# A hybrid decoder block on one core: the gate columns of the input projection as seven token-major half products, handed on through DRAM

## The reference

```python
h = rmsnorm(x, mix_pre_g)
proj = h @ w_in                       # 2048 -> 1024 + 1024 | 1024 | 4096
a_in, b_in, gates = split(proj)       # GLU input | pooling input | gates of both branches
a = a_val * sigmoid(a_gate)           # then causal depthwise conv, 31 taps
a = silu(layernorm(conv(a)))
y_a = a @ w_a_out                     # 1024 -> 2048
mixed = per-group linear map of (trailing mean - token) of b_in
y_b = (mixed * pool_scale) @ w_b_out  # 1024 -> 2048
merged = sigmoid(gates_a) * y_a + sigmoid(gates_b) * y_b
x = x + rmsnorm(merged @ w_o, mix_post_g)
...
```

## Time and profile before

| | us |
|---|---|
| runs | 2543.63, 2544.37, 2546.49 |
| median | 2544.37 |
| profiled execution, its span | 2544.4 |
| TensorE busy in it | 2498.3 (98%) |
| VectorE, ScalarE, GpSimd busy | 1922.4, 1053.4, 193.7 |

### The profile page before, as it was taken

How to read it: one execution, slowest core, us unless ns; L and a number is a source line. 1 busy time by engine, 2 the same in 40 slices (tenths; PEclk the granted TensorE clock), 3 DMA queues, 4 the chain that set the end, 5 groups by cost and what they waited for, 6 DMA issues and landing times. The chain is left out here.

```text
span 2544.4 us, 35985 instructions
## 1 busy us (share of the span) xinstructions
PE 2498.3 (98%) x14180; PEld 2193.4 (86%) x14180; DVE 1922.4 (76%) x2289; ACT 1053.4 (41%) x1224; POOL 193.7 (8%) x273
## 2 busy tenths in 40 slices
PE   9999999999999999999999999999999999999998
PEld 7788888888888787899999999999987878877886
DVE  7888766653335788889989998899988787788434
ACT  5222322252224445444444444444454453455323
POOL 0000000000000000011111111011111111200000
PEclk9999999999999999999999999999999999999999
DMA  4322333234334564467777776777787777976221
GB/s 170 106 101 91 100 99 99 91 123 134 99 99 148 166 216 181 152 196 207 211 187 213 215 218 204 195 207 210 222 269 238 262 237 192 278 228 226 89 99 67
DMA packets 155602, 435.48 MB, mean 171 GB/s; under 512 B 13504, under 2 KB 49344, under 8 KB 154432
## 3 DMA queue, kind: packets, MB, share of 16 engines
q1 hardware_dynamic: 120400, 304.12, 34.4%
q0 software_dynamic: 32656, 124.80, 20.3%
q10 hardware_dynamic: 2400, 4.53, 0.5%
HBM read 396.44 MB, written 36.96 MB: 170 GB/s over the span
## 5 line engine op out<-in xcount | busy, mean ns | idle before, releaser
L1259 ACT ACTIVATE w_hi<-ring_raw 128x1024 fp32r<-128x1024 f32 x426 | 450.6, 1060 | 606.6 <-PE ps L1144 388.0
L1762 DVE TENSOR_TENSOR ring_lo<-ring_raw,w_hi 128x1024 fp32r<-128x1024 f32 x426 | 518.6, 1222 | 190.5 <-ACT w_hi L1259 188.5
L873 PE MATMUL ps<-xg_hi,w_hi 128*128 128x512 f32 x1024 | 401.3, 392 | 7.7 <-DVE w_lo L1721 4.1
L1721 DVE TENSOR_TENSOR w_lo<-w_raw,w_hi 128x1024 fp32r<-128x1024 f32 x160 | 195.1, 1223 | 282.5 <-ACT w_hi L1239 282.3
L874 PE MATMUL ps<-xg_lo,w_hi 128*128 128x512 f32 x1024 | 399.6, 390 | 0.0
L875 PE MATMUL ps<-xg_hi,w_lo 128*128 128x512 f32 x1024 | 399.6, 390 | 0.0
L1142 PE MATMUL ps<-s_hi,w_hi 128*128 128x256 f32 x1280 | 362.3, 283 | 2.4 <-issue 2.4
L1144 PE MATMUL ps<-s_hi,ring_lo 128*128 128x256 f32 x1280 | 362.5, 283 | 0.0
L1143 PE MATMUL ps<-s_lo,w_hi 128*128 128x256 f32 x1280 | 362.1, 283 | 0.0
L1239 ACT ACTIVATE w_hi<-w_raw 128x1024 fp32r<-128x1024 f32 x160 | 168.8, 1058 | 390.3 <-PE ps L875 353.9
L1142 PE MATMUL ps<-xg_hi,w_hi 128*128 128x256 f32 x960 | 271.2, 282 | 0.6 <-DVE ring_lo L1762 0.6
(11 more groups left out here) (284 smaller groups left out, 4360.8 us busy)
## 6 DMA issues: line engine op xcount, KB each, us to landing
ring_raw<-in_w_up SPq DMA_DIRECT2D x200, 512.0 KB, 4.7
ring_raw<-in_w_down SPq DMA_DIRECT2D x114, 512.0 KB, 4.5
w_raw<-in_w_in SPq DMA_DIRECT2D x110, 512.0 KB, 3.2
ring_raw<-in_w_up POOLq DMA_DIRECT2D x80, 512.0 KB, 5.9
out_raw<-in_w_o SPq DMA_DIRECT2D x48, 512.0 KB, 4.2
ring_raw<-in_w_ple_gate SPq DMA_DIRECT2D x32, 512.0 KB, 3.5
xd_raw<-gx_dram POOLq DMA_DIRECT2D x14, 1024.0 KB, 10.6
gx_dram<-g_sums POOLq DMA_DIRECT2D x44, 256.0 KB, 7.9
```

The lines of the kernel that those rows point to most:

```text
L873: pe.matmul(o, w_hi[:, s, cols], hi, start=start, stop=False)
L1259: f(w_hi[:, (U_S + n) % SLOTS], raw_of(n), ACT.Copy).then_inc(hi_ready, 1)
L1721: dve.tensor_tensor(w_lo[:, s], w_raw[:, u.slot(RAW)], as_f32(w_hi[:, s]), ALU.subtract).then_inc(lo_ready, 1)
L1762: dve.tensor_tensor(low_of_unit(n), raw_of(n), as_f32(w_hi[:, (U_S + n) % SLOTS]), ALU.subtract).then_inc(lo_ready, 1)
```

## The change

The 4096 gate columns are taken out of `w_in` as `w_gates`, laid out like `w_o`. They are computed in four groups (`GATE_GROUPS`) of two column blocks of 512 with the seven products over halves of the contraction, of the columns and of the tokens: per group 28 units (7 products by 4 units of K), each of 12 token-major matmuls. The two units of the pooled map stand after the first four. The operand sums of x (`x_sum`) are made in place in `xt_raw`, scaled by ScalarE in stage B (`scale_x`) and split into `xs_hi`, `xs_lo`. The weight sums T1, T2, T3 are made by GpSimd with `tensor_tensor` over 128x1024 (for the first group T1 by a DMA that adds), T4 by VectorE. VectorE puts the products together in `gate_parts` (six operations per group), ScalarE takes sigmoids with the row factor `rstd_x` as scale and stores 512 KB pieces in `gates_dram` through its own DMA queue; the result of the pooled map goes through `mixed_dram`. Then come the two branch products, token-major: side 0 (B) and side 1 (A), each four column blocks of four units of 24 matmuls. VectorE multiplies each block by gates read back by GpSimd's queue (1 MB each) into `mtok`, and TensorE transposes `mtok` back (64 transposes of 128x128), which ScalarE copies to `merged`. Nothing changes from the out stage on except where in the list of the first 14 units VectorE's and ScalarE's sums stand, and which semaphores are used.

```diff
-U_B = U_A + 4 * HC
-U_M1 = U_B + 2 * HC + 2
...
+def gate_units(h):
+
+    if h == 0:
+        units = [(GATE, h, W11, q) for q in range(4)] + [(POOLED, n) for n in range(2)]
+        units += [(GATE, h, W21, q) for q in range(4)] + [(GATE, h, mat, q) for q in range(4) for mat in (T1, T2, T4)]
+    else:
+        units = [(GATE, h, mat, q) for q in range(4) for mat in ((W11, T1, T2, T4) if q < 3 else (W11, T2, T1, T4))]
+        units += [(GATE, h, W21, q) for q in range(4)]
+    return units + [(GATE, h, mat, q) for q in range(4) for mat in (T3, W22)]
...
+MIX_HOME = [j % GATE_RING if j < N_GATES else (j - N_GATES) % BRANCH_RING for j in range(N_MIX)]
...
 @block.sync
+            def mix_free(j):
+
+                home, before = MIX_HOME[j], MIX_BEFORE[j]
+                if before is not None:
+                    sp.wait_ge(units_done, U_M + before + 1)
...
 @block.gpsimd
+            def gate_sums(h, q):
+
+                first = gate_landed(h, T1, q)
+                if h == 0:
+                    pool.wait_ge(first_gate_added[q], 16)
+                else:
+                    pool.tensor_tensor(first, first, gate_landed(h, W11, q), ALU.add).then_inc(gate_sum, 1)
+                    pool.wait_ge(gate_sum, gate_summed(h, T1, q))
+                second = gate_landed(h, T2, q)
+                pool.tensor_tensor(second, second, first, ALU.add).then_inc(gate_sum, 1)
...
+            for k in range(4):
+                pool.wait_ge(gate_out[k], 16 * (GATE_GROUPS if k < 2 else 2))
+            gates_back(0, 0)
+            gates_back(0, 1)
...
 @block.tensor
+                for kk in range(2):
+                    k, cols = 2 * q + kk, slice(kk * W, (kk + 1) * W)
+                    for b in range(2):
+                        hi, lo = gate_x(mat, k, slice(b * P, (b + 1) * P))
+                        o = ps[:, bank + b]
+                        pe.matmul(o, hi, w_hi[:, s, cols], start=k == 0 and not onto, stop=False, skip_group_check=onto)
+                        pe.matmul(o, lo, w_hi[:, s, cols], start=False, stop=False, skip_group_check=onto)
+                        mm = pe.matmul(o, hi, w_low[:, cols], start=False, stop=k == HC - 1, skip_group_check=onto)
...
+            def turn_branch(n):
+
+                pe.wait_ge(mtok_ready, BLK * (n + 1))
+                for q in range(4):
+                    for b in range(BLK):
+                        mm = pe.transpose(ps[:, 4 * (n % 2) + q, b * P:(b + 1) * P], mtok[:, n, b, q * P:(q + 1) * P], ident[:])
...
 @block.scalar
+            def x_sum_high(k):
+
+                half, tok = ((upper, far), (lower, near), (lower, far), (upper, near))[k]
+                if half == lower:
+                    for n in range(2):
+                        act.wait_ge(mixed_out[n], 16)
...
 @block.vector
+                if c >= 4:
+                    x_sum(c - 4)
...
+                if j >= N_GATES - 4:
+                    mixed_low(j - N_GATES + 4)
+                elif j >= end_of_map + 4 and tap < 3 * CONV_W:
+                    conv_taps(HC // 2 + 1 + tap // CONV_W, tap % CONV_W, tap % CONV_W + 1)
+                    tap += 1
...
-            out_sum_2()
-            step(At(U_O - 1))
-            out_sum_1()
             for j in range(O_UNITS - 2):
...
-                if j == 1:
+                if j == 2:
+                    out_sum_2()
+                if j == 3:
+                    out_sum_1()
+                if j == 4:
                     late_low(near, 1)
```

More of the change, by code:

```diff
@@ L444, in build @@
         ple_taken, y_ready = sem("ple_taken"), sem("y_ready")
-        x_back, x2_out = [sem(f"x_back{k}") for k in range(2)], sem("x2_out")
+        x2_out = sem("x2_out")
         x2_in = [sem(f"x2_in{n}") for n in range(NG)]
@@ L1021, in _, with gate_x @@
-            with pe.Fori(1, 3) as i:
-                for j in range(4):
-                    branch(At(U_M1 + 3 * j, i, 12), At(T_M1 + 2 * j, i, 8), mixed_hi, mixed_lo)
+            def gate_x(mat, k, tok):
+                far = slice(TOKH + tok.start, TOKH + tok.stop)
+                return {W11: (xg_hi[:, k, tok], xg_lo[:, k, tok]), W21: (xg_hi[:, HC + k, tok], xg_lo[:, HC + k, tok]),
+                        T4: (xg_hi[:, HC + k, far], xg_lo[:, HC + k, far]), T1: (xs_hi[:, HC + k, far], xs_lo[:, HC + k, far]),
+                        T2: (xs_hi[:, k, tok], xs_lo[:, k, tok]), T3: (xs_hi[:, k, far], xs_lo[:, k, far]),
+                        W22: (xs_hi[:, HC + k, tok], xs_lo[:, HC + k, tok])}[mat]
@@ L1025, in mean @@
+            for j in range(N_GATES):
+                if MIX[j][0] == GATE:
+                    gate_unit(j)
+                else:
+                    pool_map(j)
             def mean():
@@ L1033, in variance @@
                 for b in range(BLK):
-                    mm = pe.matmul(ps[:, 4, b:b + 1], acc[:, b * P:(b + 1) * P], ones[:, 0:1], start=True, stop=True)
+                    mm = pe.matmul(ps[:, 6, b:b + 1], acc[:, b * P:(b + 1) * P], ones[:, 0:1], start=True, stop=True)
                 mm.then_inc(sums_done, 1)
-            for m in range(12, DC):
-                branch(At(U_M1 + 3 * m), At(T_M1 + 2 * m), mixed_hi, mixed_lo, within_gate=(lambda: spread(2, 7)) if m == DC - 1 else None,
-                       ahead_of_branch={12: mean, 14: variance}.get(m))
@@ L1048, in _ @@
+            for side in range(2):
+                for n in range(NG):
+                    branch(side, n)
             out_hi = {mat: (lambda k, tok, m=m_hi[mat]: m[:, k, tok]) for mat in m_hi}
@@ L2003, in _, with x_sum_low, gate_second @@
-            op.leave(3, per, start=1)
+                if c >= 4:
+                    x_sum(c - 4)
+            def x_sum_low(k):
+                half, tok = ((upper, far), (lower, near), (lower, far), (upper, near))[k]
+                dve.wait_ge(xs_hi_ready, k + 1)
+                low(xs_lo[:, half, tok], xt_raw[:, half, tok], xs_hi[:, half, tok], xs_split)
+            def gate_second(h):
+                dve.wait_ge(gate_copied, h + 1)
+                if h > 0:
+                    dve.wait_ge(gate_out[2], 16 * h)
+                dve.wait_ge(units_done, U_M + MIX_AT[GATE, h, T2, 3] + 1)
+                dve.tensor_tensor(gate_part(2), by_halves(gate_pair(h, T2)), gate_part(3), ALU.subtract).then_inc(gate_taken, 1)
@@ L2004, in _ @@
+            for tap in range(tap, 3 * CONV_W):
+                conv_taps(HC // 2 + 1 + tap // CONV_W, tap % CONV_W, tap % CONV_W + 1)
             op.settle()
```

764 lines of the change are left out of this document (521 added, 243 removed).

## The result

The changed kernel takes 2581.07 us (median of four runs, 2579.62 to 2583.03) against 2545.28: the ratio is 1.0145, interval 1.013 to 1.0159. It is 36 us **slower**, where 2535.5 was forecast with a range from 2519 to 2562. The profiled execution has a span of 2579.1 us.

The account below looks back on a forecast made before the run. TensorE alone was taken to bound the mix stage. From 2544.4 us, -32.9 (TensorE's work), +26.9 (handovers) and -3 (output projection) gave 2535.4, stated as 2535.5, with a range from 2519 to 2562.

Parts of the forecast that it names:

- TensorE's own work, -32.9: Mix stage: fewer gate matmuls gain 41.0 us, token-major branch products cost 1.5 and new transposes 6.6; net -32.9 us.
- VectorE's work in a group, 63.0: Gate groups: splits, T4 sums, taps and recombinations take VectorE 63.0 of 76.8 us, leaving 13.8 to spare.
- hidden at 2.4: Gate groups: GpSimd's sums, 2.4 us each, two per four units of 11.0 us, are ready in time.
- rival 1: Gate groups: VectorE and GpSimd take turns on SBUF, adding 10 to 31 us, middle 20; 2555.5 us, chance 0.37.
- The handovers, 26.9: Four places in the mix stage where TensorE stalls: 15.9 us of waits plus 11.0 of slower clock.
- (a): Into the pooled map: sums of x ahead of the splits delay its first unit; stall 2.3 us, clock 1.7.
- (b): Behind the map: ScalarE's second sum of x awaits the result's stores, delaying the first T2; stall 3.3 us, clock 2.5.
- (c): Into side 0: the first branch unit's buffer is freed late, so its load is late; stall 4.4 us, clock 3.4.
- (d): Side 0: gates return through DRAM at 30.6 us, their bank is wanted at 24.7; stall 5.9 us, clock 3.4.
- The output projection, -3: Output projection: later sums and earlier `merged` win 3 us of the 4.5 wait and 3.4 clock, bounds -7 and 0.
- nothing is added: Whole kernel: the profiled execution's span equals the median of the runs, so the forecast total gets no correction.
- rival 3: Gate groups: a GpSimd sum is as slow as a DMA of its size, splits wait; 2546 to 2560 us, chance 0.10.

Follow-up runs that it names:

- the cut sums: Changed kernel with GpSimd's 44 sums working on only 8 of 1024 columns, semaphores, loads and order kept; 2541.71 us, ratio 0.9996.
- the sums on VectorE: Changed kernel with the 44 weight sums made by VectorE instead of GpSimd, ahead of the splits that need them; 2542.47 us, ratio 1.0004.
- the joined kernel: The kernel whose 44 sums VectorE makes, with branch buffers turned, map result stored elsewhere and several steps moved, all at once; 2517.90 us, ratio 0.9897.
- joined kernel with GpSimd's sums: All the handovers mended together, but the 44 sums left on GpSimd as in the changed kernel; 2551.56 us, ratio 1.0036.

## Why the prediction was wrong, step by step

- **TensorE's own work, -32.9: right.** A group takes 76.6 to 76.7 us where it has its operands (76.8 forecast), and a set of 16 transposes 1.67 us (781.52 to 783.19 in the trace of after).
- **VectorE's work in a group, 63.0: right.** 64.04 us with the cut sums.
- **The price of a sum on GpSimd, 2.4: right.** The shortest of the 44 take 2.35 us; on VectorE they cost 1.79 us each in the mean.
- **GpSimd's sums "hidden at 2.4": the step that failed.** The forecast put what they cost VectorE at nothing; they cost the groups 38.4 us. Its reason, in rival 1, was "nothing in this trace shows that the two hinder each other", by which the forecast got 0.40 and the rival 0.37. A trace in which GpSimd has no work of this kind can't show that, so it was no evidence at all. In the runs the two do hinder each other: 2.89 us for a tap of 0.74, 1.23 us at most for a recombination with one input in PSUM, 1222 ns for splits beside GpSimd's writes. The one source that spoke on it beforehand was the Trainium skill (SBUF, State Buffer; Who interferes with whom), by which a VectorE instruction with two inputs in SBUF contends with a GpSimd instruction that reads SBUF. The traces agree, with the 2.89 and the 3.42 us above.
- **The size of rival 1, +20 (10 to 31): too small.** Measured 38.4 in the groups. The middle groups exceeded by 9.1 and 8.0, inside the 8 to 15 of the working, at its low end. Wrong were the deductions. The first group was taken to lose nothing, since it has eight sums: it lost 9.2. And the 7.9 us of taps that run out gave nothing back in the last group, which lost 12.1, the most of all. Its waits are 7.1 us, of which 4.24 lie at 567.8, 10 us into the group: lateness that VectorE brings along from the third group, while the last tap comes at 616.3, when the group is more than half over. The granted clock is 0.68 in the 7 us behind that wait. The working had no term for the clock that this lateness costs.
- **The handovers, 26.9: near in size, but partly by luck.** In the run with the cut sums (the forecast's own case) the mix stage lasts 30.6 us more than the one before less 32.9: 23.0 of waits and some 8 of clock, where 15.9 and 11.0 were forecast. (a) 2.3 forecast, 2.6 measured; (b) 3.3, 4.1; (c) 4.4, 4.9; (d) 5.9, but only 0.5 here and up to 1.1 in the other runs. The gates came back about as late as worked out (with the sums on VectorE they landed 30.8 us into side 0, and TensorE went on at 32.1; 30.6 forecast for the latter). But TensorE got there late as well, behind waits in side 0 that were not on my list, for the last recombination (1.2) and the mean (1.8), and the slower clock behind the wait of (c). Not on the list either were the first group's recombination (4.8 us) and the variance (2.8). These 10.6 us stand in for the 5.4 that (d) did not take. Each hangs on a step of VectorE in the new order; with the mean and the variance one unit later, the first wait is gone in the joined kernel and the second is 1.4.
- **The output projection, -3: not there.** The wait of 4.46 us stays in the changed kernel (4.45 us at 893.80), and a new one of 2.17 comes before it (883.54). The long one comes in two lengths without an edit there: 4.4 to 4.5 us in five of the runs, 2.9 in four (the cut sums among them); what decides between them is open. The new one is in every run. The long wait is gone in the joined kernels alone, where ScalarE's copy stands ahead of its split. From the output projection to the end the changed kernel takes 1732.0 us, against 1731.9 before; with the cut sums it takes 1728.8, but the kernel before was itself 2.3 us faster in that group of runs than beside the changed kernel.
- **The total without rival 1: inside its range, by terms that offset each other.** 2535.5 forecast (2527 to 2545), 2541.7 measured with the cut sums. Of the 6.2 us between them, 3.7 are the handovers. Another 1.8 is the sentence "nothing is added": in every run since, the time is 1.8 us above the profiled span of the same execution, and that the span before (2544.4) equalled the median was chance.
- **Two small errors of the working.** With 0.232 for a token-major matmul the net is -25.7 by its own prices, not -27, and in rival 3 "0.8 x 5" should be four quarters. Neither touches the result.

## What to carry to other kernels

An idle engine is not free room: before work goes to GpSimd, ask what VectorE does at that time, and from where it reads. If VectorE works on operands in SBUF and has less to spare than GpSimd's instructions last, the work is cheaper on VectorE itself (1.14 us a sum, against 1.8 that one on GpSimd took from it here). And an absence in a trace is evidence only where the trace had a chance to show the thing.

A change that gives TensorE 33 us gives them to nobody until the seams of the new order have some lead: here the seams ate 23 to 25 us of waits and some 8 of clock, and most of it was had back by another order of buffers, another place for one result and some steps moved by a few units, with no work taken out.

## What the runs showed of the hardware

- A sum of GpSimd (two operands in SBUF) and VectorE's splits, taps and sums in SBUF exclude each other, both ways: VectorE's tap of 0.74 us is recorded with 2.89, GpSimd's sum of 2.35 with up to 5.07 (joined kernel with GpSimd's sums, at 467.92 us, where a tap, a sum and a split of VectorE, 467.70 to 470.72, go first). The time stands in the record's duration, so busy shares count it as work: VectorE's "85.73 of 85.80" was 64 us of work.
- A VectorE instruction with one input in PSUM doesn't take part (1.23 us at most for six recombinations that lie wholly inside a sum of the changed kernel), nor do GpSimd's writes of constants (527 ns for 128x512, with VectorE's splits over them at 1223). A `tensor_scalar` with one operand in SBUF does: 2.43 us instead of 0.54.
- Thirty-two DMAs of 512 KB on GpSimd's queue that add land in 8.0 us at a DMA share of 0.84, eighty in the kernel before in 5.9 at 0.72 (1000 to 1900 us). The plain loads beside the former take 5.5 us, against 4.3 where there are four that add instead of thirty-two.
